# Feed-forward output steps of a float32 decoder trunk: high and low left tiles joined in one matmul, VectorE's work reordered

## What is computed

```python
D_MODEL = 1024; SEQ = 512; DEPTH = 2; D_FF = 2816

def swiglu(h, w_in, w_out):
    gate, up = jnp.split(h @ w_in, 2, axis=-1)
    return (jax.nn.silu(gate) * up) @ w_out

for layer in range(DEPTH):
    x = x + 0.5 * swiglu(rmsnorm(x, norm_ffn1[layer]), w_ffn1_in[layer], w_ffn1_out[layer])
    h = rmsnorm(x, norm_mix[layer])
    x = x + (retention(h, ...) if layer % 2 == 0 else dsa_attention(h, ...))
    x = x + 0.5 * swiglu(rmsnorm(x, norm_ffn2[layer]), w_ffn2_in[layer], w_ffn2_out[layer])
return rmsnorm(x, final_norm)
```

## Time and profile before

| | |
|---|---|
| median of 3 runs | 1927.34 us (1926.14 to 1927.45) |
| the profiled execution | 1926.12 us, of it 1924.1 us in the span |
| TensorE matmuls busy | 1906.3 us, 99% of the span |
| VectorE busy | 1591.0 us, 83% |
| ScalarE busy | 992.2 us, 52% |
| GpSimd busy | 188.8 us, 10% |
| chain that ended last | 91% TensorE, 4% VectorE, 1% each ScalarE, issue, DMA, GpSimd |

### The profile page before, as it was taken

The page is one execution under the profiler, slowest core; times in us unless marked ns, Lnnn a source line. Parts: engine busy times, 40 slices in busy tenths (PEclk is TensorE's granted clock), DMA queues, the critical chain, the costliest instruction groups (busy, mean ns, idle before and its releaser), DMA issues.

```text
span 1924.1 us, 27006 instructions
## 1 busy us (share of the span) xinstructions
PE 1906.3 (99%) x10772; PEld 1664.5 (87%) x10772; DVE 1591.0 (83%) x1905; ACT 992.2 (52%) x1298; POOL 188.8 (10%) x164
## 2 busy tenths in 40 slices
PE   9999999999999999999999999999999999999998
PEld 7888899888888888888899888889997898888998
DVE  8988896986767859889896988989768768988985
ACT  6554555452434435545655555564568445555642
POOL 0000000000000032000000000000036440000000
PEclk9999999999999999999999999999999999999999
DMA  6776855231313333677845576784422018667852
GB/s 232 197 214 214 234 188 195 105 137 44 137 44 137 107 112 91 216 197 201 270 145 180 178 234 181 206 268 140 177 85 88 1 45 261 199 190 201 264 183 86
DMA packets 100524, 316.63 MB, mean 165 GB/s; under 512 B 5936, under 2 KB 14128, under 8 KB 97328
## 3 DMA queue, kind: packets, MB, share of 16 engines
q1 hardware_dynamic: 82704, 222.35, 32.5%
q0 software_dynamic: 17408, 92.28, 19.4%
q10 hardware_dynamic: 288, 0.29, 0.1%
HBM read 312.80 MB, written 94.37 MB: 212 GB/s over the span
## 4 chain that ended last, share of the span: by engine, by line
PE 91%; DVE 4%; ACT 1%; issue 1%; DMA 1%; POOL 1%; SPq 0%; DVEq 0%; POOLq 0%; ACTq 0%
PE bank L2855 13%; PE bank L2857 13%; PE bank L2856 13%; PE bank L3028 7%; PE bank L3030 7%; PE bank L3029 7%; PE bank L2847 4%; PE bank L2849 4%; PE bank L2848 4%; PE bank L3084 3%; PE bank L3086 3%; PE bank L3085 3%; PE bank L2961 2%; PE bank L3095 1%; PE bank L3347 1%
## 5 line engine op out<-in xcount | busy, mean ns | idle before, releaser
L1212 ACT ACTIVATE part_hi<-quad_w 128x1024 fp32r<-128x1024 f32 x280 | 293.2, 1064 | 278.5 <-PE bank L2857 195.8
L1825 DVE TENSOR_TENSOR part_lo<-quad_w,part_hi 128x1024 fp32r<-128x1024 f32 x280 | 329.8, 1217 | 23.6 <-ACT part_hi L1212 23.4
L2855 PE MATMUL bank<-part_hi,s_hi 128*128 128x512 f32 x640 | 252.5, 394 | 0.7 <-DVE part_lo L1825 0.6
L2857 PE MATMUL bank<-part_hi,s_lo 128*128 128x512 f32 x640 | 249.6, 390 | 0.0
L2856 PE MATMUL bank<-part_lo,s_hi 128*128 128x512 f32 x640 | 249.3, 390 | 0.0
L2855 PE MATMUL bank<-part_hi,xn_hi 128*128 128x512 f32 x608 | 237.6, 391 | 0.8 <-DVE part_lo L1877 0.8
L2857 PE MATMUL bank<-part_hi,xn_lo 128*128 128x512 f32 x608 | 236.7, 389 | 0.0
L2856 PE MATMUL bank<-part_lo,xn_hi 128*128 128x512 f32 x608 | 236.7, 389 | 0.0
L1992 DVE TENSOR_TENSOR quad_w<-quad_w,quad_w 128x1024 f32<-128x1024 f32 x160 | 188.5, 1216 | 1.1
L1239 ACT ACTIVATE part_hi<-quad_w 128x1024 fp32r<-128x1024 f32 x84 | 87.0, 1058 | 148.5 <-PE bank L2849 105.9
L2857 PEld LDWEIGHTS bank<-part_hi,s_lo 128*128 128x128 f32 x640 | 120.1, 188 | 25.2
(11 more groups left out here) (411 smaller groups left out, 5023.3 us busy)
## 6 DMA issues: line engine op xcount, KB each, us to landing
quad_w<-w_ffn_in SPq DMA_DIRECT2D x80, 1024.0 KB, 7.5
t_sums<-w_ffn_out POOLq DMA_DIRECT2D x48, 1408.0 KB, 10.2
t_sums<-t_sums POOLq DMA_DIRECT2D x16, 1408.0 KB, 6.5
quad_w<-w_ret_in SPq DMA_DIRECT2D x14, 1024.0 KB, 7.5
first_raw<-w_ffn_out SPq DMA_DIRECT2D x16, 704.0 KB, 8.2
out_raw_C<-t_sums SPq DMA_DIRECT2D x12, 704.0 KB, 4.3
rest_raw<-w_ffn_in SPq DMA_DIRECT2D x32, 256.0 KB, 5.8
quad_w<-w_ret_in SPq DMA_DIRECT2D x16, 512.0 KB, 5.0
```

Source lines behind the costliest of these rows:

```text
L1212: nc.scalar.activation(in_four(part_hi[part_slot(h)]), source, copy).then_inc(part_hi_made, 1)
L1825: nc.vector.tensor_tensor(in_four(part_lo[part_slot(h)]), source, in_four(part_hi[part_slot(h)]).bitcast(FP32), ALU.subtract)\
L2855: mm(to, hi, in_four(part_hi[slot])[:, :, part], start=start, stop=False, skip_group_check=joins)
L2857: return mm(to, lo, in_four(part_hi[slot])[:, :, part], start=False, stop=stop, skip_group_check=joins)
```

## The change

Four things are done together.

1. The moving operand of a step now holds the high and the low left tile at once. All of them lie in one tensor, left_arena, and left_parts gives a two-piece view of 2 x 256 columns, so that weight-high times both is one matmul of 512 columns, written to a whole bank; weight-low times left-high stays a matmul of 256 columns into the first half. An output step thus has 11 x 2 matmuls. Only the last feed-forward's last tile of chain Z keeps the old form (one_width).
2. Every tile of a product now needs a bank of its own: chain Y has banks 0 to 3, and V and Z share the other four (upper_banks). The last group's transposed tiles go to these banks too. This brings new waits: S1T1 for "x11 P2", x11w11's third tile for gate2_summed, x12w21 for gated_stored, and the next sublayer for x_updated.
3. add_out adds the first halves of two banks, and then, linked by a semaphore, the second halves: two instructions for one.
4. VectorE's and ScalarE's orders are rewritten: P1 a, P2 and P6 are added earlier, P5 later; the first splits of retention (first_q) and of sparse attention (w_raw, in three parts, dsa_first) now stand before weight 26's high and low part, and no longer after weight 27's; the feed-forward's first rest parts come a little earlier, retention's first_s1 later.

The diff, cut to its core:

```diff
-X_ADDS = ["x11 P1 a", "x11 P1 b", "x11 P2 a", "x11 P2 b", "x22 P5 a", "x22 P5 b",
-          "x12 P6 a", "x12 P6 b", "x22 P7 a", "x22 P7 b"]
+X_ADDS = ["x11 P1 a", "x11 P1 b", "x11 P2 a", "x11 P2 b", "x12 P6 a", "x12 P6 b",
+          "x22 P5 a", "x22 P5 b", "x22 P7 a", "x22 P7 b"]
...
+    def left_parts(p, k):
+        both = sorted([left_hi_at[p % 2] + 4 * HALF_SEQ * k, left_low_at(p, k)])
+        return bass.AP(left_arena, (both[0] - arena_at) // 4,
+                       [[arena_width, P], [(both[1] - both[0]) // 4, 2], [1, HALF_SEQ]])
...
+    def upper_banks(s):
+        return (4, 5, 6, 7) if s + 1 < len(SUBLAYERS) and SUBLAYERS[s + 1] == "ret" else (6, 7, 4, 5)
     def out_bank(s, chain, dt):
-        if chain == "Z" and s == len(SUBLAYERS) - 1 and dt == OUT_TILES - 1:
-            return 6, 0
-        first = {"Y": 0, "V": 2, "Z": 4}[chain]
...
+        return dt if chain == "Y" else upper_banks(s)[dt]
```

On ScalarE, at the end of the phase:

```diff
                     square(0)
                     square(1)
+                    if following == "ret":
+                        split_ret("q", 0, 0)
+                        split_ret("q", 0, 1)
+                    elif following == "dsa":
+                        for n in range(3):
+                            raw, hi, _ = dsa_first(s + 1, n)
+                            act.wait_ge(*unit_loads(u0 + OUT_STEPS + (1 if n else 0)))
+                            nc.scalar.activation(hi, raw, copy).then_inc(first_hi_parts, 1)
                     out_high(i + 2)
                     residual(s, 2)
                     residual(s, 3)
```

On VectorE, in add_out:

```diff
-                    done = nc.vector.scalar_tensor_tensor(to, made, factor, to, ALU.mult, ALU.add)
+                    done = nc.vector.scalar_tensor_tensor(to, made[:, :, 0], factor, to, ALU.mult, ALU.add)
+                    if not one_width(s, chain, a):
+                        link(done)
+                        done = nc.vector.scalar_tensor_tensor(to, made[:, :, 1], factor, to, ALU.mult, ALU.add)
```

On VectorE, the order in the middle of the phase:

```diff
                 left_low(4, 0)
+                add_out("x12", 3, two[0], "P6", -0.5)
                 out_low(16)
                 left_low(4, 1)
                 out_low(17)
+                add_out("x12", 3, two[1], "P6", -0.5)
+                out_low(18)
                 sum_left("S4")
-                add_out("x12", 3, two[0], "P6", -0.5)
-                out_low(18)
                 out_low(19)
-                add_out("x12", 3, two[1], "P6", -0.5)
+                for piece in pieces(s, "Z"):
+                    add_out("x22", 2, piece, "P5", 0.5)
 
                 left_low(5, 0)
                 out_low(20)
```

On TensorE, in out_step:

```diff
+                    elif name == "S1T1":
+                        pe.wait_ge(x_added, x_added_count(s, f"x11 P2 {ab}"))
...
-                        mm(to, w_hi_k, left_hi_k, start=first_in, stop=False, skip_group_check=joins)
-                        mm(to, w_hi_k, left_lo_k, start=False, stop=False, skip_group_check=joins)
+                        if one_width(s, chain, dt):
+                            mm(to, w_hi_k, left_hi_k, start=first_in, stop=False, skip_group_check=joins)
+                            mm(to, w_hi_k, left_low_tile(p, k), start=False, stop=False, skip_group_check=joins)
+                        else:
+                            mm(both.rearrange("p (n t) -> p n t", n=2), w_hi_k, left_parts(p, k),
+                               start=first_in, stop=False, skip_group_check=joins)
                         done = mm(to, w_lo_k, left_hi_k, start=False, stop=last_in, skip_group_check=joins)
```

More of the change, by code:

```diff
@@ L2241, in _ @@
                 left_low(1, 1)
+                add_out("x11", 0, two[0], "P1", 0.5)
                 sum_left("S1")
@@ L2320, in _ @@
                     stream_lo(s + 1, 5)
-                    if following == "ret":
-                        for k in range(HALF_CHUNKS):
-                            first_s1(s + 1, k)
-                    elif following == "ffn":
-                        rest(s + 1, 0)
+                    if following == "ffn":
                         rest(s + 1, 1)
@@ L3015, in out_step @@
                     pe.wait_ge(w_lo_made, u0 + i + 1)
-                    to = cols(bank[n], first, HALF_SEQ)
-                    opens = name in ("x11w11", "x12w21", "S1T1") and dt == piece[0]
-                    closes = dt == piece[1] - 1
-                    joins = name in ("S2T2", "S3T3", "x22T4", "S4w22")
+                    both = bank[out_bank(s, chain, dt)]
+                    to = cols(both, 0, HALF_SEQ)
+                    opens = name in ("x11w11", "x12w21", "S1T1")
+                    joins = not opens
                     _, hi, lo = out_bufs(i)
```

145 lines of the change are left out of this document (77 added, 68 removed).

## The result

| | before | changed |
|---|---|---|
| median of the runs, us | 1926.78 (1926.14 to 1927.45, 4 runs) | 1946.61 (1944.41 to 1947.91, 4 runs) |
| profiled execution: time, span, us | 1926.12, 1924.1 | 1944.41, 1942.6 |
| mean granted TensorE clock | 0.998 | 0.994 |
| matmuls | 10772 | 9562 |

The changed kernel is slower: ratio 1.0102, 95% interval 1.0084 to 1.0119. I had forecast 1939 in a range of 1926 to 1947. The direction was right, and the time lies at the upper end of the range, where one of my rivals, the clock, had put it. The profiled execution is the fastest of the four: the others have mean granted clocks of 0.992 to 0.993, so they probably had more low clock than the trace shows, but no trace of them is kept. As in the prediction, the first to fourth layer are the four feed-forwards in order of time.

The account below looks back on a forecast made before the run. TensorE, busy 1906.3 of 1924.1 us at its upper clock, was taken as the bound; -16.1 + 10.1 + 5.9 + 6.7 + 5.0 = +11.6 on 1926.1 gave 1937.7, forecast as a 1939 us median, range 1926 to 1947.

Parts of the forecast that it names:

- one of my rivals, the clock: TensorE drops to 1.2 GHz in steps 26 and 27 after the new waits: 8 us together, 1947 us; 9%.
- rival (d): The clock rival: TensorE loses its upper clock at steps 26 and 27, 8 us together, 1947 us; 9%.
- Part 1: Output steps on TensorE: 1210 fewer matmuls at 13.3 ns each save 16.1 us; a step falls from 3.96 to 3.81.
- Part 2: VectorE's doubled additions in the new queue make step 20 wait 2.5 us in all four layers: 10.1 us lost.
- Part 3: Early next-layer splits wait for loads, delaying steps 26 and 27: 5.9 us lost before retention, 6.7 before sparse attention.
- The step-27 waits of 1.8: End of the feed-forward before retention: weight 27's low part ends at 17.3 against 15.5 due, another 1.8 us wait.
- Part 4: Seams between layers: later squares, broadcast and rest part on VectorE lose 5.0 us, between 0 and 7.
- retention's two: Seam at retention's start: squares 1.1 us later against TensorE, broadcast delayed 1.2 more by four first_s1; 2.3 together.
- the sparse attention's: Seam at the sparse attention: 1.4 us lost on the squares.
- the 1.3 us at the third feed-forward: Seam at the third feed-forward: 1.3 us lost on its second rest part.

Follow-up runs that it names:

- the run with the products apart: Changed kernel with the joined 512-column matmul cut in two again, additions, orders and splits as changed; 1954.49 us.
- the run with one place: Changed kernel with x22 P5 behind P7 b, splits back behind weight 27, and the joined matmul's moving operand one 512-column stretch (low products wrong); 1922.02 us.
- the filled run: Changed kernel with TensorE filling its waits before steps 20 and 26 with zero-weight float32 matmuls; 1942.44 us, ratio 1.0083 to the kernel before.

## Why the prediction came out as it did

The forecast of 1939 was 7.6 us too low, and the range holds the result by 0.4 us, thanks to rival (d). That (d) said 1947 is in part luck: it put 8 us at steps 26 and 27, where the clock cost 1.0, and the rest of the miss came from elsewhere.

**What bounds the kernel** was right: TensorE is busy 98% of the span, and what it waits for decides.

**Part 1**, 13.3 ns for a joined pair from two lengths of matmul, was right where the pace is 3.81 us, and the run with the products apart gives it by itself. I had taken no surcharge for the moving operand in two places, and the run with one place bears that out. I missed the second pace, 1.5 us here. No row of the kernel before shows it; it was seen only where the widths alternate.

**Part 2**, the wait at step 20, was right in place, releaser, count and size: 2.59 us against 2.5, 9.9 against 10.1. I had given the additions' doubling and the order of the queue in one walk and not said which mattered. The runs separate them: with P5 on either side of its new place the doubled additions cost TensorE nothing.

**Part 3** was right in its mechanism, the splits waiting for loads that stand late in the sync queue; both undoing the splits' place (-15.8 us) and mending the loads (step 26 on time) show it. For step 26 itself I had 4.1, and it was 4.35. In the third layer I took 6.4 us for w_dsa's landing and it was 7.8; the term was 8.8 and not 6.7. Why it took longer is open: it is issued 1.04 us after step 24 starts, as before, and 0.47 us behind the load ahead of it, where it was 0.48. The step-27 waits of 1.8 that I found no trace of at first were real, and the slow clock lay over them.

**Part 4**, 5.0 us, came to 4.0: retention's two and the sparse attention's were near the walk (the statistics matmul 0.8 later against 1.1, the broadcast 1.12 more against 1.2; 1.8 against 1.4 in the sparse attention), though part of it is a new wait for xn_lo (0.52 and 1.01 us) and not for the squares; the 1.3 us at the third feed-forward did not come (nothing there waits over 0.25 us).

**The term that was missing** is the price of an idle TensorE. I made the sum with the clock at its upper level everywhere, and gave its loss a rival's 9%, with the waits before step 26 alone as its place. It fell there, and also after waits of 2.1 and 2.6 us at step 20, where I had not thought of it: by the filled run it cost 3.0 us there and 1.0 at steps 26 and 27, 4.0 of the 6.9 that my sum for the span is short. The other 2.9 are the 1.5 of the slow pace, 1.4 of w_dsa's landing and smaller terms of both signs. The Trainium skill, page "TensorE: Matmul & The Clock Gate", section "What's actually happening", says that the throttled level is the default and activity releases it. This case's traces agree: 0.50 behind the waits in four places of the changed kernel, 1.00 behind all six filled ones; but it also stayed at 1.00 behind two unfilled waits of 2.59. Given waits of 4 to 7 us in my own sum, (d) should have been part of the forecast and not a rival to it.

## What to carry to other kernels

When fewer matmuls are bought with more work on another engine, walk that engine's queue between two deadlines: the same 2.6 us cost 13 us in one quarter of the queue and nothing in its neighbours. Work that is brought forward needs its load brought forward as well, and past the queue's waits, not only past its entries. Price a wait of TensorE of 1.5 us or more with a possible fall of the clock behind it, and look whether a later wait already covers that.

## What the runs showed of the hardware

- The granted clock fell to 1.2 GHz after 10 of 16 waits of 1.8 to 2.6 us at step 20, after two of 2.05 and 2.37 at step 26 and after all nine of 3.8 to 6.8 us there, and it fell after two waits of 1.5 us elsewhere; zero-weight float32 matmuls on 64 rows, 0.23 us each, kept it up in all six waits that they filled.
- A fall cost 1.5 us at step 20 (5.49 us against 3.98 to 4.00), and less where a later wait hid it.
- Streams of alternating 512 and 256 columns have two paces at the same granted clock, 3.81 and 3.89 us a step (394 and 399 ns, 277 and 281 ns for one matmul), and mostly keep one until something disturbs them. Streams of 256 columns alone showed one pace only.
- A moving operand read as two stretches of 256 columns ran at the same two paces, 3.81 and 3.89 us a step, as one of 512.
